# Gates of two token tiles added into DRAM by indirect transfers instead of one-hot products, with deeper rings

## What is computed

```python
top_s, top_i = lax.top_k(s, PEER_TOPK)
cand_s = top_s[:, :, 0, :, None] + top_s[:, :, 1, None, :]
cand_i = top_i[:, :, 0, :, None] * PEER_NKEYS + top_i[:, :, 1, None, :]
best_s, best_pos = lax.top_k(cand_s.reshape(T, PEER_HEADS, PEER_TOPK * PEER_TOPK), PEER_TOPK)
idx = jnp.take_along_axis(cand_i.reshape(T, PEER_HEADS, PEER_TOPK * PEER_TOPK), best_pos, axis=-1)
gate = jax.nn.softmax(best_s, axis=-1)
u = expert_u[idx]
v = expert_v[idx]
act = jax.nn.gelu(jnp.einsum('td,thkd->thk', xb, u).astype(jnp.float32), approximate=False)
return jnp.einsum('thk,thkd->td', (gate * act).astype(xb.dtype), v)
```

## Time and profile before

| | |
|---|---|
| median of 3 runs | 2641.95 us (2633.14 to 2645.84) |
| the profiled execution | 2637.98 us |
| its span, first to last instruction | 2636.1 us |
| matmuls busy, share of the span | 96% |
| VectorE, ScalarE, GpSimd busy | 60%, 39%, 19% |
| mean granted TensorE clock | 0.974 |
| bytes moved by DMA | 434 MB |

### The profile page before, as it was taken

The page is one execution under the profiler, slowest core; times in us unless marked ns, Lnnn a source line. Parts: engine busy times, 40 slices in busy tenths (PEclk is TensorE's granted clock), DMA queues, the critical chain, the costliest instruction groups (busy, mean ns, idle before and its releaser), DMA issues.

```text
span 2636.1 us, 31762 instructions
## 1 busy us (share of the span) xinstructions
PE 2519.1 (96%) x11982; PEld 2081.6 (79%) x11982; DVE 1579.1 (60%) x2604; ACT 1027.7 (39%) x1452; POOL 502.8 (19%) x363
## 2 busy tenths in 40 slices
PE   7999998999999999899999999999999999899995
PEld 6876676888888788778888888888888778777784
DVE  4365665555543577467767755556322777777777
ACT  4353443433332644543333334555422333333332
POOL 0030000000000000000011123333100755566651
PEclk9997999999999999999999999999999999999998
DMA  6223343233322222133344443546645899889994
GB/s 207 82 67 97 94 137 99 85 98 99 97 96 96 80 80 72 57 117 104 122 146 144 144 144 139 205 160 229 236 146 190 308 329 334 310 320 320 316 336 145
DMA packets 162696, 434.03 MB, mean 165 GB/s; under 512 B 17072, under 2 KB 59072, under 8 KB 161280
## 3 DMA queue, kind: packets, MB, share of 16 engines
q1 hardware_dynamic: 94896, 276.96, 31.6%
q10 hardware_dynamic: 43424, 77.60, 8.4%
q0 software_dynamic: 24240, 77.63, 7.9%
HBM read 369.21 MB, written 62.91 MB: 164 GB/s over the span
## 4 chain that ended last, share of the span: by engine, by line
PE 71%; DVE 11%; DMA 8%; issue 4%; ACT 4%; POOL 1%; ACTq 0%; DVEq 0%; SPq 0%; POOLq 0%
PE PS L272 20%; PE PS L274 20%; PE PS L273 20%; DVE WL L267 4%; DMA A<-acts 4%; DMA A<-gate_matrices 3%; DVE PS L1739 3%; PE PS L2172 3%; DVE A L1719 2%; ACT WGH L1135 1%; PE PS L1935 1%; PE PS L2072 1%; PE PS L2019 1%; PE PS L2006 1%; POOL A L822 1%
## 5 line engine op out<-in xcount | busy, mean ns | idle before, releaser
L267 DVE TENSOR_TENSOR WL<-RAW,WH 128x1024 fp32r<-128x1024 f32 x462 | 587.1, 1272 | 557.9 <-ACT WH L261 520.6
L272 PE MATMUL PS<-HH,WH 128*128 128x512 f32 x1696 | 667.4, 394 | 8.8 <-DVE HL L433 7.1
L273 PE MATMUL PS<-HL,WH 128*128 128x512 f32 x1696 | 660.8, 390 | 0.0
L274 PE MATMUL PS<-HH,WL 128*128 128x512 f32 x1696 | 660.8, 390 | 0.0
L261 ACT ACTIVATE WH<-RAW 128x1024 fp32r<-128x1024 f32 x462 | 485.2, 1051 | 247.5 <-PE PS L274 209.6
L272 PEld LDWEIGHTS PS<-HH,WH 128*128 128x128 f32 x1696 | 318.8, 188 | 79.2 <-DVE HL L433 10.3
L274 PEld LDWEIGHTS PS<-HH,WL 128*128 128x128 f32 x1696 | 318.6, 188 | 66.6
L273 PEld LDWEIGHTS PS<-HL,WH 128*128 128x128 f32 x1696 | 318.9, 188 | 63.4
L272 PE MATMUL PS<-WH,WGH 128*128 128x512 f32 x768 | 307.2, 400 | 39.4 <-DVE WGL L1723 38.6
L273 PE MATMUL PS<-WL,WGH 128*128 128x512 f32 x768 | 304.8, 397 | 0.0
L274 PE MATMUL PS<-WH,WGL 128*128 128x512 f32 x768 | 304.4, 396 | 0.0
(11 more groups left out here) (338 smaller groups left out, 3077.8 us busy)
## 6 DMA issues: line engine op xcount, KB each, us to landing
RAW<-in_peer_u SPq DMA_DIRECT2D x128, 512.0 KB, 3.5
RAW<-in_peer_v SPq DMA_DIRECT2D x128, 512.0 KB, 7.0
RAW<-in_w_ada SPq DMA_DIRECT2D x48, 512.0 KB, 3.7
gate_matrices<-A ACTq DMA_DIRECT2D x6, 4096.0 KB, 12.6
A<-gate_matrices ACTq DMA_DIRECT2D x32, 768.0 KB, 7.9
A<-acts ACTq DMA_DIRECT2D x32, 768.0 KB, 13.0
RAW<-in_ffn_up SPq DMA_DIRECT2D x44, 512.0 KB, 3.4
acts<-GATE SPq DMA_DIRECT2D x64, 256.0 KB, 2.3
```

What stands on the lines that cost most here:

```text
L267: nc.vector.tensor_tensor(WLr[:, slot(c), 0:w], RAW[:, slot(c), 0:w], WH[:, slot(c), 0:w], ALU.subtract).then_inc(sem("low_done"), 1)
L272: nc.tensor.matmul(out, L[0], R[0], start=first, stop=False)
L273: nc.tensor.matmul(out, L[0], R[1], start=False, stop=False)
L274: return nc.tensor.matmul(out, L[1], R[0], start=False, stop=last)
```

## The change

Gates now live in one DRAM tensor `gates[expert, row, token]` for 384 tokens (`DW`). The places of tokens 0 to 255 (`ZW`) are zeroed by 16 transfers during phase "up". For tiles 0 and 1 DVE computes each pick's place, and POOL adds each of the 128 picks of a tile by an indirect transfer of 128 elements, one per token; after each 16 it waits until all have landed. One-hot products remain for tile 2, in 16 groups, staged over 128 tokens and stored once. DVE takes over POOL's subtractions, in another order of steps. Groups of gates and activations have three buffers (`GROUPS`) instead of two and are requested at v % 4 == 1 instead of 2, picked rows have seven instead of six. Some semaphores are merged, without another order.

```diff
-NU = DW // 64
-NG8 = 8 * NU
+NP = ND - 1
+ZW = NP * P
+NG8 = P // 8
-SLOTS = 6
+SLOTS = 7
+GROUPS = 3
-LOWS_LISTED = (47, 59, 71, 77)
-LOWS_SHIFTED = (35, 47, 59, 71)
+LOWS_SHIFTED = (31, 44, 57, 70)
+LIST_AT = 64
 def before_gates(n):
-    return 80 + 3 * n // 4
+    return 80 + 3 * n // 2
...
+        gates_kept = nc.dram_tensor("gates", (P, P, DW), F32, kind="Internal").ap()
+        gate_list = gates_kept.rearrange("e p (t o) -> (e p t) o", o=1)
...
+            nc.gpsimd.memset(ZERO, 0.0).then_inc(sem("zero_set"), 1)
+            pool.wait_ge(sem("zero_set"), 1)
+            for n in range(16):
+                pool.wait_ge(sem("chunk_used"), FIRST["up"] + 2 * n + 1)
+                pool.dma_start(gates_kept.rearrange("e p t -> p e t")[:, 8 * n:8 * n + 8, 0:ZW],
+                               ZERO.unsqueeze(1).to_broadcast([P, 8, ZW])).then_inc(sem("gates_zeroed"), 16)
...
-            for t in range(NT):
-                pool.wait_ge(sem("places_ready"), t + 1)
-                for i in range(4):
-                    places_apart(t, i)
-            pool.wait_ge(sem("list_stored"), ND)
-            pool.wait_ge(sem("picks_listed"), 1)
-            for n in range(NG8):
-                wait(pool, "onehot_ready", n - 1)
...
+            pool.wait_ge(sem("gates_zeroed"), 16 * 16)
+            for t in range(NP):
+                pool.wait_ge(sem("gates_listed"), t + 1)
+                for u in range(PICKS):
+                    if u >= TOPK and u % TOPK == 0:
+                        pool.wait_ge(sem(f"gates_placed{t}"), 16 * u)
+                    pool.indirect_dma_start(out=gate_list, out_offset=bass.IndirectOffsetOnAxis(ap=PLACE[:, t, u:u + 1], axis=0),
+                                            in_=SHARES[:, t, u:u + 1], in_offset=None, compute_op=ALU.add)\
+                        .then_inc(sem(f"gates_placed{t}"), 16)
...
-            for r in range(2):
-                pool.wait_ge(sem(f"gates_written{r}"), 16 * NU // 2)
+            pool.wait_ge(sem("picks_listed"), 1)
+            pool.wait_ge(sem("gates_stored"), 16)
             for u in range(SLOTS):
                 pick_row(u)
...
+                if n == NG8 - 1:
+                    act.wait_ge(sem("gm_stored"), 2 * NG8)
+                    act.dma_start(gates_kept.rearrange("e p t -> p e t")[:, :, ZW:DW], STG).then_inc(sem("gates_stored"), 16)
...
                 if p == QU - 6:
-                    for r in range(2):
-                        act.wait_ge(sem(f"gates_written{r}"), 16 * NU // 2)
+                    for t in range(NP):
+                        act.wait_ge(sem(f"gates_placed{t}"), 16 * PICKS)
+                    act.wait_ge(sem("gates_stored"), 16)
...
-                if v % 4 == 2 and 2 <= v // 4 + 2 < P // 4:
-                    j = v // 4 + 2
+                if v % 4 == 1 and v // 4 + GROUPS < P // 4:
+                    j = v // 4 + GROUPS
...
-                    act.wait_ge(sem("w_done"), 4 * (j - 1))
+                    act.wait_ge(sem("w_done"), 4 * (j - GROUPS + 1))
                     load_group(j)
...
             def summed(t, i):
-                dve.wait_ge(sem("eq_ready"), 4 * t + i + 1)
+                places = PAB.rearrange("p s u -> p (s u)")[:, i * 64:i * 64 + 64].rearrange("p (h k) -> p h k", k=TOPK)
+                ranks = con("iota")[:, 0:TOPK].unsqueeze(1).unsqueeze(1)
+                link(nc.vector.tensor_tensor(EQ, places.unsqueeze(3).to_broadcast([P, PH // 2, TOPK, TOPK]),
+                                             ranks.to_broadcast([P, PH // 2, TOPK, TOPK]), ALU.is_equal))
...
-            for s_ in range(NT + 1):
-                wait(dve, "list_turned", s_ - 1)
+            for t in range(NT):
                 for i in range(4):
                     low_of_next()
-                    if s_ < NT:
-                        last = pairs(s_, i)
-                        low_of_next()
-                    if s_ >= 1:
-                        summed(s_ - 1, i)
-                        low_of_next(s_ < NT or i % 2 == 0)
...
+                    last = pairs(t, i)
+                    low_of_next(t > 0)
+                until(last)
+                shifted(t)
+                for i in range(4):
+                    low_of_next()
+                    summed(t, i)
+                low_of_next()
+                listed(t)
```

More of the change, by code:

```diff
@@ new lines, in build @@
+        GD = 4 * DW
+        G4 = A[:, 0:GROUPS * GD].rearrange("p (r i t) -> p r i t", r=GROUPS, i=4)
+        AC = A[:, GROUPS * GD:2 * GROUPS * GD].rearrange("p (r i t) -> p r i t", r=GROUPS, i=4)
+        o4 = 2 * GROUPS * GD
+        WGHr = over("A", "WGH", o4, GD, F32R).rearrange("p (r t) -> p r t", r=4)
+        WGLr = over("A", "WGL", o4 + GD, GD, F32R).rearrange("p (r t) -> p r t", r=4)
+        WGH = WGHr.bitcast(F32)
+        WF = A[:, o4 + 2 * GD:o4 + 2 * GD + 2 * DW].rearrange("p (r t) -> p r t", r=2)
@@ L644, in build @@
+        o5 = o4 + 2 * GD + 2 * DW
+        ROWS = A[:, o5:o5 + SLOTS * D].rearrange("p (r n) -> p r n", r=SLOTS)
+        assert 11264 <= o5 and o5 + SLOTS * D <= 20480
+        PLACE = over("A", "PLACE", 21504, NP * PICKS, U32).rearrange("p (t u) -> p t u", t=NP)
+        SHARES = A[:, 21760:22144].rearrange("p (t u) -> p t u", t=ND)
+        LST = A[:, 22144:22528].rearrange("p (l t) -> p l t", l=3)
+        STG = A[:, 0:16384].rearrange("p (i t) -> p i t", i=P)
         OHA = A[:, 16384:18432].rearrange("p (r n) -> p r n", r=16)
@@ L645, in build @@
         OHB = A[:, 18432:20480].rearrange("p (r n) -> p r n", r=16)
[L647 to L657, removed]
+        ZERO = A[:, 21504:21504 + ZW]
         ACC = PS[:, 2 * GT_TILE:2 * GT_TILE + 2, :]
@@ L1652, in listed @@
+                link(last)
+                link(nc.vector.tensor_reduce(N12[:, t % 2].rearrange("p s u -> p (s u)")[:, i * 64:i * 64 + 64],
+                                             EQ.rearrange("p h k a -> p (h k) a"), AX, ALU.add))
             def listed(t):
-                assert lows[0] == LOWS_LISTED[t]
                 dve.wait_ge(sem("best_exp"), t + 1)
-                dve.wait_ge(sem("eq_summed"), 4 * t + 4)
+                n1, n2 = N12[:, t % 2, 0], N12[:, t % 2, 1]
                 link(nc.vector.tensor_reduce(zg, BV[:, t % 2], AX, ALU.add))
@@ new lines, in listed @@
+                last = nc.vector.tensor_tensor(shares.rearrange("p (h k) -> p h k", h=PH), BV[:, t % 2],
+                                               zg.unsqueeze(2).to_broadcast([P, PH, TOPK]), ALU.mult)
+                if t == NP:
+                    last.then_inc(sem("list_ready"), 1)
+                    return
+                link(nc.vector.scalar_tensor_tensor(EXPERT, n2, float(P), n1, ALU.mult, ALU.add))
+                token = con("token")[:, t:t + 1].to_broadcast([P, PICKS])
+                if t < NP:
+                    nc.vector.scalar_tensor_tensor(PLACE[:, t], EXPERT, float(DW), token, ALU.mult, ALU.add)\
+                        .then_inc(sem("gates_listed"), 1)
+                else:
+                    nc.vector.scalar_tensor_tensor(A_AT, EXPERT, float(S), token, ALU.mult, ALU.add)
@@ L2178, in _ @@
                 acts(u_of(p))
-                for t in range(NT):
-                    if t < ND and p == LOWS_LISTED[t] - 2:
-                        pe.wait_ge(sem("list_ready"), t + 1)
-                        wait(pe, "list_stored", t)
-                        for l, src in enumerate((N12[:, t % 2, 0], N12[:, t % 2, 1], BV[:, t % 2].rearrange("p h k -> p (h k)"))):
-                            last = nc.tensor.transpose(PS[:, 4, l * P:(l + 1) * P], src, ident)
-                        last.then_inc(sem("list_turned"), 1)
+                if p == LIST_AT:
+                    pe.wait_ge(sem("list_ready"), 1)
+                    for l, src in enumerate((N12[:, NP % 2, 0], N12[:, NP % 2, 1], SHARES[:, NP])):
+                        last = nc.tensor.transpose(PS[:, 4, l * P:(l + 1) * P], src, ident)
+                    last.then_inc(sem("list_turned"), 1)
                 for n in range(NG8):
```

125 lines of the change are left out of this document (45 added, 80 removed).

## The result

| | before | changed |
| --- | --- | --- |
| median | 2643.89 us of 4 runs (2633.14 to 2647.19) | 2529.84 us of 4 runs (2529.24 to 2531.53) |
| profiled execution, its span | 2637.98, 2636.1 us | 2531.53, 2529.7 us |
| PE busy in the span | 2519.1 us | 2446.7 us |
| mean granted clock of TensorE | 0.974 | 0.979 |

The changed kernel takes 0.9576 of the time, 95% interval 0.9548 to 0.9605: 4.2% faster. The medians differ by 114 us, the two profiled executions by 106.5; the forecast was a difference of 105. The extra 7.6 us between medians is scatter: 5.9 us of the kernel before, 1.7 of the changed one.

A forecast was written before the change was run, and what follows sets the result against it. PE's own work and waits were taken as the bound, with DVE's late group loads holding PE up in the v stage. Savings of 57 + 48 = 105 us gave 2533 us profiled, 2537 us as median, range 2522 to 2592.

The forecast's parts named there:

- One-hot products: Between the u chunks: 32 of 48 one-hot groups fall away, 1.78 us of PE each, all on the path; -57 us.
- DVE's order in tile 0: Tile 0: DVE's added subtractions and later splits stay hidden behind PE's 5.46 us chunks; 0 us, up to 5 otherwise.
- Zeroing and the store of 8 MB: Up stage and after group 15: the zeroing transfers and the single gate store are both hidden; 0 us.
- The adds: POOL's 256 indirect adds, priced like activation gathers, take 451 us and end before ACT's wait at p = 138; 0 us.
- The upper bound of 724 us: Time for all 256 adds with each at the longest gather row; 116 us too late.
- The deadline: ACT's wait for the last add at p = 138: 608 us available, or 2.38 us per add, before PE is held.
- Group loads: v stage: three buffers and earlier requests remove all 54 us of DVE's waits; 58 us lost, 10 left, so -48 us.
- The threshold: v stage: a group load is on time if its lead, now 34.8 us, exceeds the slowest landing, 23.8 us.
- B: v stage: DMA becomes the bound at 329 GB/s, so the kernel takes 2559 us; chance 0.20.
- C: Adds miss ACT's wait: not overlapping, 5.0 us each, 3209 us, chance 0.12; mild, at longest rows, 2653 us, chance 0.05.
- D: v stage: the deeper ring is inert, DVE's 46.1 us of waits without releaser being something else; 2578 us, chance 0.05.
- The estimate of 16 us per add: Adds: 128 elements on 16 DMA engines, 8 in a row at 2 us each; some 4100 us for all.

The follow-up runs named there:

- adds_plain: The changed kernel with plain scattered writes to the same places instead of the indirect adds; 2787.38 and 2696.09 us in two runs.
- rings_undone: The changed kernel with two group buffers, requests at v % 4 == 2 and six row slots, as before; 2581.3 us, ratio 0.9767.
- rings_alone: The kernel before with only three group buffers, requests at v % 4 == 1 and seven row slots, semaphores merged for room; 2591.21 us, ratio 0.9799.
- adds_serial: The changed kernel, but POOL waits for the landing of each single add instead of after each 16; 2909.45 us in one run.
- adds_by_four: The changed kernel, but POOL waits for all landings after each 4 adds instead of each 16; 2585.29 us, ratio 0.9778.
- plain_serial: The changed kernel with plain scattered writes instead of adds, POOL waiting for each one's landing; 2719.68 us, ratio 1.0291.

## Why the prediction came out right

**One-hot products (-57 us).** 256 records remain, and the v stage starts 56.0 us earlier. Right.

**DVE's order in tile 0 (0).** DVE's timeline in tile 0, with the other operations left out:

```profile
1301.11 1.22 DVE L267 TENSOR_TENSOR WL<-RAW,WH 128x1024 fp32r<-128x1024 f32 x1
...
1306.61 1.21 DVE L267 TENSOR_TENSOR WL<-RAW,WH 128x1024 fp32r<-128x1024 f32 x1
```

A split every 5.50 us, as worked out from the earlier trace rows, against 5.46 us of PE's chunk; PE shows no wait there. Right. The first add started at 1348.3 us, some 6 us later than I had put the list's end.

**Zeroing and the store of 8 MB (0).** PE keeps its 249.11 us beside the zeroing. The store, by its line:

```profile
L1122 ACTq DMA_DIRECT2D gates<-A x1: 400/400/400, 1751.3 to 1751.3; - x1
...
DMA to landing us min/median/max: 45.5/45.5/45.5
```

It landed at 1797 us, 155 us ahead of the group loads. Right. The margin was counted too long: it left 200 us before the group loads, not 230, since these stand at p = 138 and not at the end of the phase (37 chunks of 5.46 us instead of 42).

**The adds (0, with 157 us to spare).** The sign was right and the size was not: this is the term that I mis-sized. I took the gather of activations, 1.45 us per add and 5.0 us per wait, 451 us in all; the run shows 561 us from the first add to the last, and some 39 us to spare. The waits were shorter and fewer than put (2.6 us each in 14 places, instead of 5.0 in 16: each tile has 7), the issue much longer: 1.70 us of POOL instead of 1.15 (1546 ns is the usual one), and a gap of 92.8 / 241 = 0.39 us instead of 0.30. That is (2.08 - 1.45) x 256 = 161 us more, less 80 - 36.6 = 43 us of waits. adds_plain tells where the POOL part comes from: the same instruction with no addition takes 972 ns, like the gather. "The engine and the elements are the same" was thus no sufficient reason; the transfer's kind has a price of its own, for POOL and for the DMA engines. The upper bound of 724 us still held it. The deadline came out well: 2.38 us per add was predicted, the runs bracket it, with 2.20 hidden and 2.55 late by 52.2 us.

**Group loads (-48 us).** The stage became 50.1 us shorter. Of the 58 lost, 8 are left, where I had put 10. Most of them lie at the start and the end: PE has 112.75 of 115 us up to 2100 and 97.13 of 100 behind 2400, 5.1 us in all. That the waits with no releaser were group loads rested on the loads' own rows; rings_undone shows it. The threshold that I used, the slowest load against the lead, fits the table of the four rings, although the slowest load rose from 23.8 to 25.7 us. The seventh slot for picked rows, which I counted among the ring's means, does nothing. (By the rows shown, four weight steps take 16.00 us, so a step is 4.00 us and not 3.99; this moves no lead by more than 0.1 us.)

**The rivals.** B, DMA as the bound at 329 GB/s, fell: 329 was what the kernel before asked for, not a bound. It delivered 355 to 357 GB/s beside a full PE, and 359 in rings_alone. I had the row against it, 59.18 of 60 us at 337 GB/s, and gave B 0.20 all the same. C fell in both forms, by 2.20 us per add against 3.80 for adds that do not overlap; adds_serial shows what it would have been, 2909 us, not the 3209 of the prediction, because a lone add takes 3.80 us from one to the next rather than 5.0. Its mechanism of a deadline is real, as adds_by_four shows. D fell with rings_undone.

The estimate of 16 us per add that the prediction drew from the Trainium skill's "DMA: Bandwidth & Descriptors" does not hold here: alone, an add of 128 elements of 4 bytes lands in 3.1 us (adds_serial), so it does not pay 2 us for each of 8 elements in a row. The run speaks against the 2 us only: with the 0.2 us that the page gives as the average the same estimate is 1.6 us, which would fit. What the page says about a read before the write may still be so; the packets and the engine time of an add, above, show that it is more than a write, and not what it does.

## What to carry to other kernels

When a wait names no releaser, look at what the waiting instruction reads and at the rows of its loads; then compare the slowest landing, not the median, with the lead of the request. Depth beyond that lead is worth nothing, and a few microseconds short of it can cost tens. An indirect DMA with an addition moves scattered sums off the main engine, but price it by its own kind, as issue by POOL plus waits, and count from when its list is ready to when its result is needed: here 39 of some 600 us were left. When waits are added to a stream of issues, take off the gaps that they replace.

## What was not expected of the hardware

- **Accumulating costs issue time.** POOL takes 1546 ns for an indirect add of 128 elements and 967 to 972 ns for the same write without the addition; alone they land in 3.1 and 2.1 us. The add also keeps the 16 DMA engines busy for 6.2 us in sum instead of 0.4 (the changed kernel and plain_serial).
- **Plain scattered writes, one in 1.4 us, hold up the core; adds, one in 2.2 us, do not.** With the plain writes PE ran for 191 of 374 us with DMA at 50 GB/s (adds_plain, one execution), and the hold-up came only after some 20 us of them; with one at a time, each 3.1 us, PE ran for 374 of 374 at 139 GB/s; with adds for 374 of 374 at 138 GB/s. The cause is open. A guess that was not tried is that issuing faster (1.3 us per write against 2.1 per add, waits left out) fills some queue.
- **DMA at a share of 1.00 moved 359 GB/s over 100 us** (rings_alone), a mixture of 512 KB weights, gate pieces of 1 KB and gathers, and PE was still full. The Trainium skill's "HBM Reference", section "Specifications (TRN2)", gives about 358 GB/s per core, and says that a core alone can go well above it. One core runs here, and the trace agrees with the second in stretches of 10 us, up to 407 GB/s in the changed kernel. That the average over 100 us lies at the first figure may be chance; no run here shows what large transfers alone, or two cores, would reach.
